# Inverting a 64x64 triangle in 32x32 array tiles, and moving the one-token samples' state update into the feed-forward stage behind

## The reference

```python
def decoder_layer(x, shift, wkv, sc_buf, ssm_conv, ssm, lp):
    x = x + 0.5 * swiglu(rmsnorm(x, lp['norm_ffn1']), lp['ffn1_w_in'], lp['ffn1_w_out'])
    ...
    x = x + jnp.concatenate([y_rwkv, y_sc, y_ssm], axis=-1) @ lp['w_out']
    x = x + 0.5 * swiglu(rmsnorm(x, lp['norm_ffn2']), lp['ffn2_w_in'], lp['ffn2_w_out'])

# in rwkv7_mix, for each token and head (64x64 state S):
def step(S, inp):
    r_t, w_t, k_t, v_t, kk_t, b_t = inp
    Sa = jnp.einsum('bhij,bhj->bhi', S, -kk_t)
    S = S * w_t[:, :, None, :] + Sa[..., None] * b_t[:, :, None, :] + v_t[..., None] * k_t[:, :, None, :]
    return S, jnp.einsum('bhij,bhj->bhi', S, r_t)
```

## Time and profile before

| | |
|---|---|
| three runs, median | 1665.74 us (1665.28 to 1670.03) |
| the profiled execution, first to last instruction (the time that the profile has for it) | 1667.1 us |
| PE, DVE, ACT, POOL busy | 94%, 68%, 51%, 16% of the span |
| granted TensorE clock, mean | 0.983 |

### The profile page before, as it was taken

One profiled execution on the slowest core, in us unless ns is written; L12 is line 12 of the kernel. 1 busy time (PEld: TensorE's weight loads), 2 busy tenths in 40 slices (PEclk: granted clock), 3 DMA queues, 4 the chain that ended last, 5 costly groups with the idle time before them and its releaser, 6 DMA issues. The chain is left out here.

```text
span 1667.1 us, 41414 instructions
## 1 busy us (share of the span) xinstructions
PE 1566.2 (94%) x17379; PEld 1486.8 (89%) x17379; DVE 1140.1 (68%) x1822; ACT 858.5 (51%) x1515; POOL 262.7 (16%) x259
## 2 busy tenths in 40 slices
PE   7999999989799899999999999999997989899997
PEld 6999999987688789999999999989775878799997
DVE  6565587795798667665575656968768886676654
ACT  5444464667444555444354444657673445554443
POOL 0000003001356431000000000030014554300000
PEclk9999999999899999999999999999998999999999
DMA  7555556471244545555454655644703463455552
GB/s 230 178 172 170 168 159 199 130 208 53 59 125 120 144 157 161 194 179 186 143 186 160 194 183 175 189 141 128 215 1 102 126 178 98 131 189 187 183 178 71
DMA packets 280650, 256.28 MB, mean 154 GB/s; under 512 B 48054, under 2 KB 268700, under 8 KB 280450
## 3 DMA queue, kind: packets, MB, share of 16 engines
q1 hardware_dynamic: 276698, 252.05, 48.5%
q10 hardware_dynamic: 3768, 1.59, 0.4%
HBM read 242.22 MB, written 11.38 MB: 152 GB/s over the span
## 5 line engine op out<-in xcount | busy, mean ns | idle before, releaser
L209 ACT ACTIVATE front_hi<-front_raw 128x1024 fp32r<-128x1024 f32 (+2 forms) x230 | 238.5, 1039 | 262.0 <-PE ps L234 255.5
L216 DVE TENSOR_TENSOR front_lo<-front_raw,front_hi 128x1024 fp32r<-128x1024 f32 (+1 forms) x210 | 252.2, 1201 | 109.0 <-ACT front_hi L209 108.2
L209 ACT ACTIVATE out_hi<-out_raw 128x1024 fp32r<-128x1024 f32 (+1 forms) x168 | 173.3, 1038 | 219.1 <-PE ps L234 205.1
L216 DVE TENSOR_TENSOR out_lo<-out_raw,out_hi 128x1024 fp32r<-128x1024 f32 (+1 forms) x148 | 183.9, 1243 | 108.1 <-ACT out_hi L209 107.3
L232 PE MATMUL ps<-front_h_hi,front_hi 128*128 128x264 f32 (+1 forms) x816 | 241.3, 296 | 4.9 <-DVE front_lo L216 3.3
L234 PE MATMUL ps<-front_h_hi,front_lo 128*128 128x264 f32 (+1 forms) x816 | 233.0, 286 | 0.0
L233 PE MATMUL ps<-front_h_lo,front_hi 128*128 128x264 f32 (+1 forms) x816 | 232.7, 285 | 0.0
L232 PE MATMUL ps<-ffn_h_hi,out_hi 128*128 128x264 f32 x704 | 200.7, 285 | 0.1
L233 PE MATMUL ps<-ffn_h_lo,out_hi 128*128 128x264 f32 x704 | 200.0, 284 | 0.0
L234 PE MATMUL ps<-ffn_h_hi,out_lo 128*128 128x264 f32 x704 | 199.8, 284 | 0.0
L232 PE MATMUL ps<-in_h_hi,front_hi 128*128 128x264 f32 x688 | 197.4, 287 | 0.0
(11 more groups left out here) (400 smaller groups left out, 3891.7 us busy)
## 6 DMA issues: line engine op xcount, KB each, us to landing
front_raw<-in_w_in SPq DMA_DIRECT2D x50, 1024.0 KB, 5.2
out_raw<-in_ffn_w_in SPq DMA_DIRECT2D x44, 1024.0 KB, 5.2
front_raw<-in_ffn_w_in SPq DMA_DIRECT2D x40, 1024.0 KB, 5.3
back_sample_rows<-row_scratch SPq DMA_DIRECT2D x160, 128.0 KB, 3.0
out_raw<-in_w_out SPq DMA_DIRECT2D x16, 1024.0 KB, 6.3
front_raw<-in_ffn_w_out SPq DMA_DIRECT2D x16, 896.0 KB, 4.6
out_raw<-in_ffn_w_out SPq DMA_DIRECT2D x16, 896.0 KB, 4.6
front_raw<-in_ffn_w_out SPq DMA_DIRECT2D x8, 1024.0 KB, 5.0
```

The lines of the kernel that those rows point to most:

```text
L209: act.activation(self.hi[n % self.RING][:, 0:k, 0:w], self._raw(n), ACT.Copy).then_inc(self.hi_ready, 1)
L216: eng.tensor_tensor(self.lo[n % self.RING][:, 0:k, 0:w], self._raw(n), self.hi[n % self.RING][:, 0:k, 0:w].bitcast(F32), ALU.subtract).the ...
```

## The change

First, the inverse is kept compact. Levels stop at 16, and up to there the inverse consists of 32x32 diagonal blocks alone, so `x` is stored as four 32-column blocks (`HB` = 32) per partition quarter, and `small_blocks` issues 16 products of 32x32 by 32 columns on the four diagonal 32x32 tiles of the array. The transpose of `x`, which was a running sum of its own, is now made from `x` by a DVE transpose of 32x32 blocks (`turn_blocks`), so `level_u` has one product and `update` one addition. The last level joins two 32-blocks to a 64-block with two short groups of 8 products, written straight into the 64-column `xt` by `finish` (lower half) and `upper_blocks` on ACT (upper half).

Second, the samples' state is no longer updated in the rounds. Two products of the old state are taken there (with kk, and with decay times r), summed, and the outputs are put together from them and two dot products per head that PE makes once (`rec_products`, `rec_sums`, `sample_outputs`). The update itself (`SampleUpdate`) stands in ffn2: SP loads three rows and the old state for each pair between the weight loads, POOL makes both outer products in place, and DVE does three instructions of 128x512 behind `hidden_lo` in every second step `m` from 3 to 17.

```diff
-LEVELS = (2, 4, 8, 16, 32)
+LEVELS = (2, 4, 8, 16)
+VECS = 5
+KK, REC, DEC, MB, KEY = range(VECS)
+HB = 32
...
+class SampleUpdate:
+    def sp(self, sp, n):
+        if n == 0:
+            sp.wait_ge(*self.free)
+        if n >= 2:
+            sp.wait_ge(self.done, 3 * (n - 1))
+            sp.dma_start(self.new[n - 2], self.state[(n - 2) % 3][:]).then_inc(self.stored[(n - 2) % 3], 16)
+        if n < RT:
+            for h in range(2):
+                sp.dma_start(self.rows[h * HS:(h + 1) * HS, n % 2].rearrange("p v b j -> p v (b j)"),
+                             self.row_mem[DEC:KEY + 1, 2 * n + h].rearrange("v b j -> v (b j)").unsqueeze(0).to_broadcast([HS, 3, NS * HS])
+                             ).then_inc(self.rows_in[n % 2], 16)
+            if n >= 3:
+                sp.wait_ge(self.stored[n % 3], 16 * (n // 3))
+            sp.dma_start(self.state[n % 3][:], self.old[n]).then_inc(self.state_in[n % 3], 16)
...
+    def pool(self, pool):
+        for q in range(RT):
+            pool.wait_ge(self.rows_in[q % 2], 32 * (q // 2 + 1))
+            for i, x0 in ((1, self.env.sample_sums[:, q, 0]), (2, self.env.sample_v[:, q])):
+                row = self.rows[:, q % 2, i]
+                pool.tensor_tensor(row, row, x0.unsqueeze(2).to_broadcast([P, NS, HS]), ALU.mult).then_inc(self.products, 1)
+
+    def dve(self, dve, m):
+        q = (m - 3) // 2
+        if m % 2 == 0 or not 0 <= q < RT:
+            return
+        st0 = self.state[q % 3]
+        dve.wait_ge(self.state_in[q % 3], 16 * (q // 3 + 1))
+        dve.wait_ge(self.rows_in[q % 2], 32 * (q // 2 + 1))
+        for i, op in ((0, ALU.mult), (1, ALU.add), (2, ALU.add)):
+            if i:
+                dve.wait_ge(self.products, 2 * q + i)
+                dve.wait_ge(self.done, 3 * q + i)
+            dve.tensor_tensor(st0[:], st0[:], self.rows[:, q % 2, i], op).then_inc(self.done, 1)
...
                 for p in range(3, len(pieces)):
                     ws.load(sp, p)
+                    if p >= 13 and (p - 13) % 2 == 0 and (p - 13) // 2 < RT + 2:
+                        update.sp(sp, (p - 13) // 2)
...
-                    act.activation(t1[:].rearrange("p q t -> p (q t)"), ps[:, T1B, 0:4 * C], ACT.Copy).then_inc(s("t1_in"), 1)
+                    act.activation(t1[:, :, 0:HB], ps[:, T1B, 0:4 * HB].rearrange("p (q t) -> p q t", q=4), ACT.Copy).then_inc(s("t1_in"), 1)
...
+                def upper_blocks(p):
+                    act.wait_ge(s("xt_in"), LT * (p + 1))
+                    act.activation(xt[:, p % 3, :, 0:HB], x_t[:, p % 2], ACT.Copy, scale=sides[:, 0:1]).then_inc(s("upper_in"), 1)
...
+                def turn_blocks(p):
+                    dve.transpose(flat(x_t[:, p % 2]), flat(x[:, p % 2])).then_inc(s("xt_in"), 1)
+
                 def start(p):
-                    dve.wait_ge(s("first_done"), p + 1)
-                    dve.tensor_tensor(xt[:, p % 3], xt[:, p % 3], eye2.unsqueeze(1).to_broadcast([P, 4, C]),
-                                      ALU.add).then_inc(s("start"), 1)
+                    dve.wait_ge(s("x_ps"), p + 1)
+                    dve.tensor_tensor(x[:, p % 2], four(T1B), eye32.unsqueeze(1).to_broadcast([P, 4, HB]), ALU.add).then_inc(s("x_in"), 1)
+                    dve.wait_ge(s("x_in"), p + 1)
+                    turn_blocks(p)
 
                 def update(p, i):
...
+                    dve.wait_ge(s("u_ps"), LT * p + i + 1)
+                    dve.tensor_tensor(x[:, p % 2], x[:, p % 2], four(UB), ALU.add).then_inc(s("x_up"), 1)
+                    dve.wait_ge(s("x_up"), LV * p + i + 1)
+                    turn_blocks(p)
+
+                def finish(p):
+                    dve.wait_ge(s("u_ps"), LT * (p + 1))
+                    dve.scalar_tensor_tensor(out=xt[:, p % 3, :, HB:C], in0=x_t[:, p % 2], scalar=sides[:, 1:2], in1=four(UB + 1),
+                                             op0=ALU.mult, op1=ALU.add).then_inc(s("xt_up"), 1)
...
+                def sample_products(m):
...
+                    dve.tensor_tensor(prod[:], state[:, m % 2].unsqueeze(1).to_broadcast([P, 2, NS, HS]), rows[:, m % 2],
+                                      ALU.mult).then_inc(s("sampled"), 1)
+
+                def sample_sums(m):
+                    dve.wait_ge(s("sampled"), m + 1)
+                    dve.tensor_reduce(sums[:, m], prod[:], AX.X, ALU.add).then_inc(s("summed"), 1)
...
-                def blocks(at, left, right):
+                def small_blocks(at, left, right):
                     for q in range(4):
-                        for w in half:
-                            mm = pe.matmul(ps[w, at, q * C:(q + 1) * C], left[w, q], right[w, q], start=True, stop=True)
+                        for i, w in enumerate(quarter):
+                            mm = pe.matmul(ps[w, at, q * HB:(q + 1) * HB], left(w, q, in_block[i % 2]), right(w, q), start=True, stop=True)
                     return mm
...
```

More of the change, by code:

```diff
@@ L333, in act_hi @@
     def act_hi(self, act, k):
+        if k == 0 and self.update is not None:
+            self.update.wait_stored(act)
         act.wait_ge(self.x_ready, k + 1)
@@ L403, in pool @@
                 self.ws.split_lo(pool, n)
+        if self.update is not None:
+            self.update.pool(pool)
     def act(self, act):
@@ L474, in dve @@
                 self.side.dve(dve)
+            if self.update is not None:
+                self.update.dve(dve, m)
         hidden_lo(FT - 1)
@@ L2119, in _ @@
                     if 0 <= l < RT:
-                        step(l, 5)
-                        update(l, 4)
-                        step(l, 6)
-                        step(l, 7)
+                        finish(l)
+                    if g < RT:
+                        start(g)
                     if g == RT - 1:
```

265 lines of the change are left out of this document (135 added, 130 removed).

## The result

The changed kernel takes 1705.1 us (median of four runs, 1696.0 to 1711.6) against 1666.7 (1665.3 to 1670.0) for the kernel before beside it: a ratio of 1.0224, with a 95% interval of 1.0187 to 1.0261. The prediction was 1630 us, and slower had a chance of 6%. The profiled execution of the changed kernel spans 1708.8 us, 41.7 more than that of before.

The account below looks back on a forecast made before the run. PE's work in its fixed order bounds the round: 13.3 instead of 15.7 us saves 38 us over 16 rounds, 36 after round 1 gives some back. 1667.1 less 36 is 1631, the median 1.4 lower: 1630 us, range 1614 to 1656.

Parts of the forecast that it names:

- The sum of the round: In each round: the hops sum to 12.8 us, with 0.5 kept for gaps 13.3 instead of 15.7 us.
- gaps inside groups that no semaphore explains; I keep 0.5: In each round: PE's pauses inside groups, 0.4 us above the best round in the mean before, put at 0.5 us.
- DVE in the rounds: DVE's busy time in a round falls from 13.4 of 15.7 us to about 8 of 13.3, not a bound.
- cost nothing, up to 1 us for each pair: SP's queue in ffn2: a pair's traffic and two weight pieces take 11.0 of 11.6 us, so it fits, just.
- Rival (2): ffn2's queue needs 12.6 us instead of 11.6; PE waits 1 us for seven pairs in both layers; 1644 us, chance 0.10.
- signs of being wrong: x32 groups over 0.45 us, DVE releasing a gap ahead of `level_t1` over 1 us, or PE in ffn2 awaiting a split.
- PE has two banks in hand: cost nothing: In ffn2: splits come about two halves early, so DVE's update of 2.0 to 3.5 us each time costs PE nothing.
- (3): In `small_blocks`: diagonal 32x32 tiles don't run side by side; at 30 ns, 3.75 us a round slower, 1726 us; chance 0.04.
- (1): In the inverse's groups: small records stay at 14.7 ns; 11 us of gain remain, 1655 us; chance 0.12.
- (4): In the rounds: DVE's order holds the hops' length, nothing gained; 14.8 us and more, 1660 to 1671; chance 0.06.
- (5): In the rounds: shapes cost nothing where PE waits, gaps go with row traffic; 12.0 us a round, 1607; chance 0.08.
- The Trainium skill's floor of about 25 ns between matmul starts: In the inverse: 320 records would take 8.0 us, the round 2.1 us longer in PE's work; 1699 us, 1 in 100.

Follow-up runs that it names:

- e5: The kernel before with four bursts of products without a wait at the head of layer 0's back stage, run once; instructions came at 128 records in 3.7 us.
- e3: The change with `turn_x` and the first four `level_t1` as 8 products of 64x64 by 32 columns instead of 16 of 32x32; 1670.6 us.
- e10: e3 with the columns doubled in all its small groups, the second result not used; 1658.7 us.
- e9: The change with each product of the 32x32 groups over 64 columns instead of 32, the second half not used; 1700.4 us.
- e1: The change with the samples' state updated in the rounds as before, so the compact inverse alone; 1687.0 us.
- e8: The change with `turn_x`, `level_t1` and `level_u` as 64x64 products, transposes spread with zeros by DVE, and the samples' state updated in the rounds; 1682.6 us.
- e2: The change with the inverse of before, so the moved samples' update alone; 1676.0 us.
- e12 to e17: Apart from e13, five kernels: e3 or e10 with parts of the moved update's loads, stores or arithmetic in ffn2 left out; ratios to before 0.9963 to 1.0017.
- e11: e3 with the samples' state updated in the rounds as before instead of moved to ffn2; 1660.2 us.
- e13: e11 with doubled columns in all small groups; 1658.2 us.

## Why the prediction was wrong

**The sum of the round was right at full clock and without gaps.** Records 9.4 ns (8.8), a group with its shape 0.39 us, the DVE transpose 0.31 us (0.28), the 128x1024 product 1.43 and its sum 1.18 us (1.2 each), a round 13.6 us (13.3):

```profile
1386.30 0.31 DVE L2060 STREAM_TRANSPOSE back_inverse_blocks_t<-back_inverse 128x128 f32<-128x128 f32 x1
...
1390.31 1.43 DVE L2104 TENSOR_TENSOR back_prod<-back_sample_wkv,back_sample_rows 128x1024 f32<-128x1024 f32 x1
...
1393.13 1.18 DVE L2109 TENSOR_REDUCE sample_sums<-back_prod 128x16 f32<-128x1024 f32 x1
```

**The failed step is "gaps inside groups that no semaphore explains; I keep 0.5".** It carried the gaps of before over to a kernel with 80 more records a round at a third of the spacing. They are 2.5 to 2.8 us a round. At e5's pace 517 records take 517 / 128 x 3.7 = 14.9 us, more than the 13.3 that was forecast; the 437 of before take 12.6. The average isn't all: of the 15 gaps over 0.9 us twelve end 1.7 to 6.6 us ahead of a `turn_x` and one lies in it, late in the round, where small groups follow each other closely, and the packets that end them come later than at that pace. The gap of the earlier trace rows, which the prediction left alone, ends 2.7 us behind a packet as the others do, with half clock behind it: the mechanism could be seen in the trace of before.

**The second failure is a term that the sum did not have: the clock.** Nothing was said of what the smaller work would do to it. Seven rounds at 13.6 us are 95.2 us; with the gaps of 19.8 and 17.3, 17.3 and 18.8 us are left for 51 and 58 us at 1.2 GHz, a third of a microsecond for each. That third, taken to others, gives e3 95.2 + 7.1 + 9 = 111 us (112.0 measured), e10, with 4.9 us more of columns, 95.2 + 4.9 + 6.9 + 3.4 = 110.4 (110.4), and e9, with 10.5 more, 132 (130.8). The third is a subtraction and not a measurement of its own, but it holds for three kernels, and for e1 with the samples' steps in its rounds (95.2 + 16.9 + 11.4 = 123.5 in layer 1, 123.5 measured); e3 itself has a round of 13.6 us at full clock, with 0.3 us of gaps. e10 against e3 shows that the columns in the records move the clock, at equal records and gaps, and e8 that a fall needs no issue gap. The gaps have a share as well, as far as times tell: in the change all five half-clock stretches of layer 1's rounds, and six of the eight in layer 0, begin inside an issue gap or at most 1.5 us behind one. How much of the 51 and 58 us is theirs stays open.

**DVE in the rounds.** Near in size (65 us of 132, 9.3 a round; predicted 8), and worth nothing: e1 has 86 us of DVE work and rounds that are no longer, e2 has before's inverse and rounds no shorter. PE bounded them, as the prediction itself said; the move had no gain to bring, only its price.

**ffn2 "cost nothing, up to 1 us for each pair".** The queue was read rightly as near full (predicted near 0.9; 0.91 in the window shown), and a weight piece lands in 9.2 us instead of 5.2. Rival (2) comes nearest: over the kernels with the move the price is 4 to 12 us in all, inside the bound of 1 us a pair. PE's waits in the change's ffn2 are for the splits and for `hidden` on DVE (L466), not for a weight piece; the first three lines are layer 0's, the last is layer 1's:

```profile
PE ps L237 <- DVE ffn_inner L466: 3.2, 3, 1.5
PE ps L237 <- DVE out_lo L221: 2.2, 1, 2.2
PE ps L237 <- ACT out_hi L214: 1.7, 2, 1.0
...
PE ps L237 <- DVE out_lo L221: 2.6, 1, 2.6
```

That PE waits for a split in ffn2 was one of the prediction's own signs of being wrong: "PE has two banks in hand: cost nothing" failed too. Whether the splits are late by the queue or by DVE is what e12 to e17 left open.

**The rivals.** (3), slower by tiles not running side by side, was the right sign with the wrong mechanism: the diagonal tiles do run side by side. (1), 14.7 ns, is out. (4), hops that DVE's order holds, is out as well: PE waited 2.7 us for `update` in all of layer 1's seven rounds. In (5) the gaps were to go with the row traffic; the DMA share fell from 0.53 to 0.30 and the gaps grew. The Trainium skill's floor of about 25 ns between matmul starts, weighed in the prediction, does not hold for the groups on four tiles (9.4 and 14.7 ns); those on two (28 and 30) lie above it, and so does the pace over hundreds of records in e5 (29). Read as a bound on the round instead of on a group, it would have given 517 x 25 = 12.9 us, an estimate from that page, and still not the loss.

## What to carry to other kernels

Count the instructions of a stretch, not only the columns: where the profile shows idle time by "issue" inside groups, measure the pace at which instructions come, and see whether the new round fits under it. When work on PE gets smaller, the clock is a term of the sum: compare the granted clock of the stretch in the two traces, and try fewer, wider products; here even useless columns paid. And a load taken off an engine that doesn't bound the stretch brings nothing, while its new place has a price: here e3's inverse is faster without the move (e11, 0.9958 against 1.0026).

## What was unexpected of the hardware

- PE's instructions came in packets of 128 records (16 KB), in the bursts one in 3.7 us (3.45 to 4.0), after 155 and 279 records had run without a gap; this held at 1.2 and 2.4 GHz. In the bursts and in the kernels' rounds every standstill over 0.9 us that was looked at ended 2.2 to 2.9 us behind the start of such a packet.
- 50 us of 64x64 by 32-column products without a gap ran at 1.2 GHz to the end; four-tile products with 1.4 to 1.9 us of standstill every 3.7 us held 2.4 GHz.
- On two 64x64 tiles 32 columns cost as much as 64 (28 and 30 ns a record); four 32x32 tiles with 32 columns take 9.4 ns. The Trainium skill (TensorEngine Tiling (Array Packing), Performance Considerations, Instruction Overhead) says that very short free dimensions save nothing; the two-tile rows agree. The four 32x32 tiles do not: a group of 32 records starts 0.39 us before the next with 32 columns and 0.58 with 64 (e9).
- Doubling the columns of every small product made a kernel 0.8% faster (e10 against e3) and another 0.3% (e13 against e11).
